# Down stage of a one-layer diffusion step: the order of its first loads, a fourth activation slot, and the multiplication by the gate row before the root

## What is computed

```
def ffn_sublayer(x, shift, scale, gate, g_pre, g_post, w_gate, w_up, w_down):
    h = rms_norm(x, g_pre) * (1 + scale) + shift
    f = (jax.nn.silu(h @ w_gate) * (h @ w_up)) @ w_down
    return x + gate * rms_norm(f, g_post)
```

## Time and profile before

| | us |
|---|---|
| runs | 1767.3, 1766.49, 1763.88 |
| median of the runs | 1766.49 |
| the profiled execution, device time | 1768.09 |
| its span (first to last instruction) | 1766.3 |
| mean granted TensorE clock in it | 0.982 of full |

### The profile page before, as it was taken

How to read it: one execution, slowest core, us unless ns; L and a number is a source line. 1 busy time by engine, 2 the same in 40 slices (tenths; PEclk the granted TensorE clock), 3 DMA queues, 4 the chain that set the end, 5 groups by cost and what they waited for, 6 DMA issues and landing times. The chain is left out here.

```text
span 1766.3 us, 24765 instructions
## 1 busy us (share of the span) xinstructions
PE 1677.5 (95%) x9795; PEld 1500.1 (85%) x9795; DVE 1040.2 (59%) x1581; ACT 725.2 (41%) x1208; POOL 74.6 (4%) x116
## 2 busy tenths in 40 slices
PE   6999899999799999999997999999999998999997
PEld 6787788878678888887887999999999997888885
DVE  5855765328755555574568554555545554467777
ACT  5652323334544444463564333333333333434453
POOL 0100000004300000000000000000000000000000
PEclk9999999999999999999999999999999999999998
DMA  9134242002400000114321222222222225573345
GB/s 370 70 131 139 108 147 75 25 33 54 119 14 19 1 13 1 66 37 156 124 96 37 100 86 84 91 88 93 95 82 85 101 76 194 187 234 97 121 145 196
DMA packets 76290, 176.33 MB, mean 100 GB/s; under 512 B 10352, under 2 KB 26944, under 8 KB 74128
## 3 DMA queue, kind: packets, MB, share of 16 engines
q1 hardware_dynamic: 72080, 169.75, 27.7%
q0 software_dynamic: 4096, 5.01, 0.9%
HBM read 131.02 MB, written 43.70 MB: 99 GB/s over the span
## 5 line engine op out<-in xcount | busy, mean ns | idle before, releaser
L409 PE MATMUL psF<-gv,gu_ring 128*128 128x320 f32 x1232 | 382.5, 310 | 9.2 <-issue 4.6
L410 PE MATMUL psF<-gv,gu_ring 128*128 128x320 f32 x1232 | 382.0, 310 | 0.0
L411 PE MATMUL psF<-gv,gu_ring 128*128 128x320 f32 x1232 | 382.0, 310 | 0.0
L409 PEld LDWEIGHTS psF<-gv,gu_ring 128*128 128x128 f32 x1232 | 232.5, 189 | 10.1 <-issue 9.1
L410 PEld LDWEIGHTS psF<-gv,gu_ring 128*128 128x128 f32 x1232 | 232.4, 189 | 0.0
L411 PEld LDWEIGHTS psF<-gv,gu_ring 128*128 128x128 f32 x1232 | 232.3, 189 | 0.0
L409 PE MATMUL psF<-d_w_ring,d_hid_ring 128*128 128x512 f32 x360 | 141.4, 393 | 6.3 <-DVE d_w_ring L2687 6.3
L410 PE MATMUL psF<-d_w_ring,d_hid_ring 128*128 128x512 f32 x360 | 141.6, 393 | 0.0
L411 PE MATMUL psF<-d_w_ring,d_hid_ring 128*128 128x512 f32 x360 | 141.4, 393 | 0.0
L409 PE MATMUL psP<-hT_hi,win_hi 128*128 128x512 f32 (+1 forms) x336 | 122.9, 366 | 2.3 <-DVE hT_lo L184 1.6
L411 PE MATMUL psP<-hT_hi,win_lo 128*128 128x512 f32 (+1 forms) x336 | 119.7, 356 | 0.0
(11 more groups left out here) (425 smaller groups left out, 3622.2 us busy)
## 6 DMA issues: line engine op xcount, KB each, us to landing
hid_variants<-hraw SPq DMA_DIRECT2D x77, 320.0 KB, 2.2
d_hid<-hid_variants SPq DMA_DIRECT2D x77, 320.0 KB, 3.0
m_wring<-in_w_mod SPq DMA_DIRECT2D x16, 1024.0 KB, 5.5
d_b<-in_w_down SPq DMA_DIRECT2D x44, 256.0 KB, 3.8
win_raw<-in_w_in SPq DMA_DIRECT2D x18, 512.0 KB, 5.7
w_mod_staged<-in_w_mod SPq DMA_DIRECT2D x16, 512.0 KB, 11.8
raw_gu<-in_w_gate SPq DMA_DIRECT2D x11, 512.0 KB, 3.9
raw_gu<-in_w_up SPq DMA_DIRECT2D x11, 512.0 KB, 4.8
```

What stands on the lines that cost most here:

```text
L409: pe.matmul(out, w_hi, x_hi, start=first, stop=False, skip_group_check=onto)
L410: pe.matmul(out, w_hi, x_lo, start=False, stop=False, skip_group_check=onto)
L411: return pe.matmul(out, w_lo, x_hi, start=False, stop=last, skip_group_check=onto)
```

## The change

- `hr` gets a fourth slot (HR = 4), in memory that held odd gate weights in the stage before; the load of e = 3 therefore waits for the last low part of that stage (`wv_lo`, NQ), and loads from e = 4 on wait for the low parts of step e - 4.
- The seven stores of the last pair go from before the load of e = 3 to before the load of e = 5.
- The four row loads go from before the load of e = 4 to one before each of the loads of e = 11, 12, 13 and 14.
- The five early finishes are at (5, 4), (5, 6), (5, 7), (5, 9), (6, 1) instead of (5, 5), (5, 7), (5, 9), (6, 1), (6, 3); `store_out` stands eight steps behind instead of seven.
- A tile's values are multiplied by the row first (`by_row`, two operations on 512 columns, which don't need the root), and `finish` is one operation on 1024 columns: value * root + x. For tiles 5 to 9 the second halves are multiplied as soon as their slot is free, the first halves behind `add`.

```
-    hr = at("d_hid", 8 * SLOT, [P, 3, TH])
+    HR = 4
+    hr_home = at("d_hid", 8 * SLOT, [P, 3, TH])
+    hr_more = at("d_hid_more", o_ring + 12288, [P, TH])
+    hr = [hr_home[:, i, :] for i in range(3)] + [hr_more[:]]
...
-        FINISH = [(5, 5), (5, 7), (5, 9), (6, 1), (6, 3)]
+        FINISH = [(5, 4), (5, 6), (5, 7), (5, 9), (6, 1)]
...
-                if e == 3:
+                if e == HR - 1:
+                    sp.wait_ge(wv_lo, NQ)
+                if e >= HR:
+                    sp.wait_ge(h_lo, e - HR + 1)
+                    sp.wait_ge(w_lo, e - HR + 1)
+                if e == HR + 1:
                     sp.wait_ge(prod, 2 * q_of(FT - 1, 6) + 2)
                     store_pair(FH - 1)
-                if e == 4:
-                    load_rows()
-                if e >= 3:
-                    sp.wait_ge(h_lo, e - 2)
-                    sp.wait_ge(w_lo, e - 2)
+                if FH <= e < FH + 4:
+                    load_row(e - FH)
...
-                sp.dma_start(hr[:, e % 3, :], L.hv[s, f]).then_inc(hr_loaded[e % 3], 16)
+                sp.dma_start(hr[e % HR], L.hv[s, f]).then_inc(hr_loaded[e % HR], 16)
...
+            def load_row(i):
                 c = slice(5 * D, 6 * D)
...
+                src = (L.gate_rows[0:1, c], L.gate_rows[1:2, c], L.dram["b_mod"][:, c], L.dram["g_post_ffn"])[i]
+                dst = rows[:, i, :] if i < 2 else out[:, i - 2, :]
+                sp.dma_start(dst, src.to_broadcast([P, D])).then_inc(row_loaded, 16)
...
-                if divmod(e - 7, FH) in FINISH:
-                    store_out(FINISH.index(divmod(e - 7, FH)))
+                if divmod(e - HR - 4, FH) in FINISH:
+                    store_out(FINISH.index(divmod(e - HR - 4, FH)))
...
-                act.wait_ge(hr_loaded[e % 3], 16 * (e // 3 + 1))
+                act.wait_ge(hr_loaded[e % HR], 16 * (e // HR + 1))
...
+            def by_row(t, i):
                 u, late, g = t % HT, t >= HT, int(t >= NT_LAT)
-                dve.wait_ge(rs_r, t + 1)
                 if t >= 3:
                     dve.wait_ge(stored[t % 3], 16 * (t // 3))
...
+                if late and i == 1:
+                    dve.wait_ge(v_made, HT + u + 1)
+                else:
+                    dve.wait_ge(c_done, t + 1)
+                half = slice(512 * i, 512 * i + 512)
+                x = ((acc_d, acc_a), (acc_b, acc_c))[i][late]
+                dve.tensor_tensor(out[:, t % 3, half], x[:, u, :], rows[:, g, half], ALU.mult).then_inc(fi_yt, 1)
+                scaled.append(t)
+
+            def finish(t):
+                dve.wait_ge(rs_r, t + 1)
+                dve.wait_ge(fi_yt, max(i + 1 for i, x in enumerate(scaled) if x == t))
                 dve.wait_ge(y_loaded[t % 2], 16 * (t // 2 + 1))
-                dve.tensor_tensor(out[:, t % 3, :], out[:, t % 3, :], yin[:, t % 2, :], ALU.add).then_inc(y_r, 1)
+                dve.scalar_tensor_tensor(out[:, t % 3, :], out[:, t % 3, :], f_rs[:, t:t + 1], yin[:, t % 2, :],
+                                         ALU.mult, ALU.add).then_inc(y_r, 1)
...
+            for t in range(HT, HT + 3):
+                by_row(t, 1)
             for t in range(HT, NT):
                 add(6, t - HT)
-                if t > HT and t < NT - 1:
+                if HT < t < NT - 1:
                     finish(t - 1)
+                by_row(t, 0)
                 mean(t)
+                if HT + 3 <= t + 1 < NT:
+                    by_row(t + 1, 1)
             finish(NT - 2)
             finish(NT - 1)
```

More of the change, by code:

```diff
@@ L2136, in phase_mix_ffn @@
              "u3_read", "c11", "c22", "c12", "silu1", "silu2", "hid1", "hid2", "hs_made", "hs_stored"))
-        hr_loaded = [L.sem(f"dn_hid_loaded{i}") for i in range(3)]
+        hr_loaded = [L.sem(f"dn_hid_loaded{i}") for i in range(HR)]
         wd_loaded = [L.sem(f"dn_w_loaded{i}") for i in range(4)]
@@ L2319, in load_d @@
                     sp.dma_start(b12[:, f, :], L.dram["w_down"][f][:, 512:1024]).then_inc(b12_loaded[f], 16)
-            def load_rows():
+            def load_row(i):
                 c = slice(5 * D, 6 * D)
[L2323 to L2326, removed]
+                src = (L.gate_rows[0:1, c], L.gate_rows[1:2, c], L.dram["b_mod"][:, c], L.dram["g_post_ffn"])[i]
+                dst = rows[:, i, :] if i < 2 else out[:, i - 2, :]
+                sp.dma_start(dst, src.to_broadcast([P, D])).then_inc(row_loaded, 16)
             def store_out(t):
@@ L2456, in highs @@
                     act.wait_ge(dprod, HT * (e - 2))
-                act.wait_ge(hr_loaded[e % 3], 16 * (e // 3 + 1))
+                act.wait_ge(hr_loaded[e % HR], 16 * (e // HR + 1))
                 if e == NE - LATE:
                     act.wait_ge(t4_made, FH)
-                act.activation(ring_h(e, 0), hr[:, e % 3, :], ACT.Copy).then_inc(h_hi, 1)
+                act.activation(ring_h(e, 0), hr[e % HR], ACT.Copy).then_inc(h_hi, 1)
                 if s < 3:
@@ L2683, in lows @@
                 dve.wait_ge(h_hi, e + 1)
-                dve.tensor_tensor(ring_h(e, 1), hr[:, e % 3, :], ring_h(e, 0).bitcast(F32), ALU.subtract
+                dve.tensor_tensor(ring_h(e, 1), hr[e % HR], ring_h(e, 0).bitcast(F32), ALU.subtract
                                   ).then_inc(h_lo, 1)
@@ L2819, in mean @@
                 dve.tensor_scalar(f_ms[:, t:t + 1], f_ms[:, t:t + 1], 1.0 / D, EPS, ALU.mult, ALU.add).then_inc(ms_r, 1)
-            def finish(t):
+            scaled = []
+            def by_row(t, i):
                 u, late, g = t % HT, t >= HT, int(t >= NT_LAT)
-                dve.wait_ge(rs_r, t + 1)
                 if t >= 3:
                     dve.wait_ge(stored[t % 3], 16 * (t // 3))
[L2826 to L2830, removed]
+                if late and i == 1:
[9 more added lines that the diff above has]
+                dve.wait_ge(fi_yt, max(i + 1 for i, x in enumerate(scaled) if x == t))
                 dve.wait_ge(y_loaded[t % 2], 16 * (t // 2 + 1))
-                dve.tensor_tensor(out[:, t % 3, :], out[:, t % 3, :], yin[:, t % 2, :], ALU.add).then_inc(y_r, 1)
+                dve.scalar_tensor_tensor(out[:, t % 3, :], out[:, t % 3, :], f_rs[:, t:t + 1], yin[:, t % 2, :],
+                                         ALU.mult, ALU.add).then_inc(y_r, 1)
             for e in range(NE):
@@ L2851, in _ @@
                 if (s, f) in FINISH:
-                    finish(FINISH.index((s, f)))
+                    t = FINISH.index((s, f))
+                    by_row(t, 0)
+                    by_row(t, 1)
+                    finish(t)
+            for t in range(HT, HT + 3):
+                by_row(t, 1)
             for t in range(HT, NT):
                 add(6, t - HT)
-                if t > HT and t < NT - 1:
+                if HT < t < NT - 1:
                     finish(t - 1)
+                by_row(t, 0)
                 mean(t)
+                if HT + 3 <= t + 1 < NT:
+                    by_row(t + 1, 1)
             finish(NT - 2)
```

## The result

The changed kernel takes 1751.68 us, median of four runs (1750.7 to 1753.38), against 1766.66 for the kernel before beside it. The ratio is 0.9919, 95% interval 0.9902 to 0.9936: 11.3 to 17.3 us less. Forecast were 1749.9 and a range of 1746.5 to 1757.0. The profiled execution took 1751.78, with a span of 1749.94, 16.3 less than the 1766.28 of before.

The account below looks back on a forecast made before the run. TensorE, busy 1677.5 of 1766.3 us, bounds the kernel; gains 10.0 + 3.65 + 3.0 = 16.65 take the profiled 1768.09 to 1751.45, and 1.6 less for a median gives 1749.9. Range 1748.3 to 1756.0, with run spread 1746.5 to 1757.0.

Parts of the forecast that it names:

- First loads: Start of the down stage: loads issued sooner remove both stops and their slow clock, gain 10.0 us, bounds 8 to 10.
- second rival: Start of the down stage: a stop before step 5 instead of step 3, price 3.9 us, 1753.8 us; chance 0.10.
- Row loads: Steps 11 to 14: one row load before each step's load fits into free DMA time, cost 0.
- third rival: Steps 11 to 14: row loads stall TensorE, slower; passes the gain and 0.2% at 6.3 us per row; chance 0.04.
- the cover that four slots give: Steps 11 to 14: time a load may fall behind before TensorE stops, forecast as 5.5 us.
- Last loads: Last five steps: of 4.86 us lost, a 1.2 us stop stays without clock fall; gain 3.65, bounds 1.8 to 4.86.
- first rival: End: last load still costs the clock, x of tile 9 late; gain 13 to 14.5 us, 1752 to 1753.4; chance 0.20.
- Tail: Behind the last matmul: VectorE ends after 4.4 us instead of 7.57; gain 3.0 after 0.2 lost, bounds 0.7 to 3.4.
- GpSimd's power lies beside the first of the two: Tail: GpSimd's power runs alongside the first of the last two `finish` operations, each 1.285 us.
- The room: Tail: time from issue to need of the load of tile 9's x, 4.1 us; landings 4.0 to 6.5, median 4.9.
- Sum: Whole kernel: gains of 10.0, 3.65 and 3.0 us add to 16.65.
- the forecast's band: Whole kernel: gains of 15 to 18.2 us, times of 1748.3 to 1751.5 us; chance 0.62.

Follow-up runs that it names:

- e5: The changed kernel with all four row loads before the load of step 11; one run, 1744.01 us (kernel before: 1761.29).
- e4: The changed kernel with three `hr` slots instead of four; median 1752.38 us, ratio 0.9929 to the kernel before.
- e3: The changed kernel with all four row loads before the load of step 6; one run, 1754.23 us (kernel before: 1761.29).
- e7: The changed kernel with tile 4's store and its x load behind the last load, step 76's; one run, 1751.21 us (kernel before: 1761.29).
- e8: The kernel before with only the new multiplication order (`by_row`, `finish`); median 1763.16 us, ratio 0.9989 to the kernel before.
- e10: The changed kernel with stores and row loads back at their old places, fourth slot kept; one run, 1761.41 us (kernel before: 1764.03).
- e1: The changed kernel with finishes, their places and operations as before the change; median 1751.97 us, ratio 0.9929 to the kernel before.
- e6: The changed kernel with the seven stores back before the load of step 3; one run, 1752.58 us (kernel before: 1761.29).
- e11: The changed kernel with three slots and tile 4's store behind the last load; median 1749.06 us, ratio 0.9913 to the kernel before.
- e2: The changed kernel with the root multiplied first, `finish` of three operations; median 1752.82 us, ratio 0.9935 to the kernel before.

## Why the prediction was right

**The mechanism held step by step.** TensorE lost time in three places, and the change won in each nearly what was forecast. At the start and in the tail the experiments show the cause; at the last loads several parts of the change act together.

*First loads: 10.0 forecast, 10.0 measured.* Step 3's load was issued at 1470.74 (forecast near 1470.4), no stop stands between steps 2 and 5, and step 5's load, behind the stores now, was there when ScalarE wanted it. One step of the forecast was wrong and cost nothing: step 3's load was to need at most 3.57 us and took 6.54, behind other loads, and still landed at 1477.28, 5.1 us before its use. The second rival (the first stop only moves to step 5) is out.

*Row loads: 0 forecast, 0 measured.* The third rival is out as well. e5 shows a row to hold the queue for about 1.7 us, within the bounds of 1.6 to 2.5 and far from the 6.3 of the rival. My reason for the 0 was too narrow, though: I counted on the cover that four slots give, and e4, with three, has no stop there either.

*Last loads: 3.65 forecast, 3.9 measured.* The place and the cause of the stop that was to stay were right, one stop at step 76 behind a pair of store and x load. Mis-sized was the time I carried over from before, 7.79 us from the store's issue to ScalarE: 7.46 here, and 6.2 to 7.3 in the five other executions with the same order of the queue, three of which had no stop at all. It scatters by more than the whole stop, so that the 3.9 came so near to 3.65 is in part luck. TensorE was 0.85 us late instead of 1.2, and the clock stayed at 1.00, which puts the first rival's fall out.

My reason for no fall was weak. I compared 1.2 with single stops of 0.84 and 1.98 and named one stop of 1.51 in the kernel before. There were two, and the clock fell behind them:

```profile
1739.47 0.47 PE L409 MATMUL psF<-d_w_late,d_hid_late 128*128 128x512 f32 x1 [1.00 <-DVE d_w_late L2687]
```

```profile
1740.30:1743.70 3.40, 3.40 (x10) 2.63 (x9) 1.00 (x3) 0.92 (x4) 0.55 (x1) 0.50 0.01 2
```

So some 1.6 of the 4.86 us that the last five steps lost before was the clock, and this place was nearer to a fall than I gave it.

The section of the Trainium skill weighed in the prediction (TensorE: Matmul & The Clock Gate, "A second HAM failure mode: psum-queue depth-cycling") tells of a kernel whose frequent short idles between groups of matmuls make the clock swing. I had read it as a rule for the one stop at step 76, and as such the traces don't bear it out: they have 1.00 behind the 0.69 us here and behind the 1.50 of e3. Whether the falls behind the pairs of stops in the kernel before and in e4 (0.52) are what that section describes is not shown.

*Tail: 3.0 forecast, 2.7 measured.* The failed step is a small one: "GpSimd's power lies beside the first of the two." It began beside it, but spanned 1.57 us against the operation's 1.28, so the second `finish` was 0.44 us late: the whole difference between 4.82 and the 4.4 forecast. The 0.2 that I had put there for the x of tile 9 was right in size (0.19), but hidden by that wait; in e7, e8 and e10 the x came with waits of 0.96, 1.24 and 1.36. The room was as forecast (4.1 us; 4.2 here and in e7); landings near 5 us lie on either side of it. VectorE waits for no store in the trace, as forecast of `by_row`.

*Sum: 16.65 forecast, 16.65 in the stage, 16.3 in the span* (the stage began 0.3 later). That the sum agrees to the last digit is luck, as the last loads' part scatters by a microsecond. That the median fell by 15.0 only, and lies 1.8 above the forecast, is the last step: I took the profiled execution's 1.6 above its median over to the changed kernel, whose profiled execution lies 0.1 above its own. By the time alone, 1751.68 stands between the forecast's band (up to 1751.5) and the first rival's (from 1752); the traces decide between them.

## What to carry to other kernels

Where TensorE waits for a load, look first at what stands before that load in the issuing queue: ten of these sixteen microseconds came from putting stores and row loads that nobody needed yet behind loads that were, and a buffer more gave next to nothing there. A buffer more can help where a load's issue waits for an earlier step's work; the end of the stage points to that, with one trace of each kernel. A stop that turns out at a microsecond is decided by how a load's landing scatters, so take such a term as a range, and remove the wait rather than shorten it.

## What the runs showed of the hardware

- **Clock.** Stops of 0.47 (e5), 0.69 and 1.50 us (e3) alone, of 0.42 and 1.01 with two microseconds between their ends (e1), and of 0.54, 0.40 and 1.01 in a row (e8) left the granted clock at 1.00. Stops of 1.98, 2.33 (e6) and 2.39 us (e11), and pairs of 1.51 and 1.00 (before) and of 1.86 and 1.02 (e4), about two microseconds between their ends, came with windows at 0.50 to 0.63. The length alone doesn't decide: step 3 of e10 ran at 1.00 behind a stop of 2.59 us. What does is open here.
- **One load behind the same pair of transfers** on the same queue came after 6.2 to 7.5 us in six executions of the same order (the change, e2, e3, e5, e6, e10), and after 7.79 in the kernel before.
- **GpSimd's power of one column** spans 0.55 to 1.57 us. The last of the stage takes 1.00 us in the three executions with the old operations of `finish` (before, e1, e2) and 1.57 in the ten with the new. e2 differs from the change in nothing else, so it is VectorE's work beside it that counts; what in that work makes the power slow was not tested.
